# A gated delta rule's heads on one core: modulation rows spread over the chain, the next head's keys ahead of the former head's squares

## What is computed

```python
mod = c_act @ ada_w[layer] + ada_b[layer]        # 6 x 1024 values for each layer
h = rmsnorm(x, g) * (1.0 + scale_m) + shift_m
qkv = silu(conv(h @ w_in)); k = l2norm(k); q = l2norm(q) * 128 ** -0.5
L = where(strict, (k * beta) @ k.T * decay, 0)   # chunks of 64 tokens
u = solve(L + I, v * beta); w = solve(L + I, k * beta * exp(g_cum))
attn = (q @ k.T) * decay
def step(S, ...):                                 # the chain over chunks
    v_new = u_i - w_i @ S
    o_i = q_i @ S + a_i @ v_new
    S = S * gl_i + k_i.T @ v_new
o = rmsnorm(o, norm_g) * silu(gate)               # then o @ w_out
```

## Time and profile before

| what | value |
|---|---|
| median of 3 runs | 2258.55 us (2256.09 to 2258.67) |
| profiled execution, its time | 2256.59 us |
| profiled execution, its span | 2254.8 us |
| PE busy | 2159.7 us, 96% of the span |
| DVE, POOL, ACT busy | 1173.2, 1216.9, 604.2 us |
| mean granted TensorE clock | 0.987 |
| PE's share of the chain that ended last | 86% |

### The profile page before, as it was taken

The page is one execution under the profiler, slowest core; times in us unless marked ns, Lnnn a source line. Parts: engine busy times, 40 slices in busy tenths (PEclk is TensorE's granted clock), DMA queues, the critical chain, the costliest instruction groups (busy, mean ns, idle before and its releaser), DMA issues.

```text
span 2254.8 us, 29386 instructions
## 1 busy us (share of the span) xinstructions
PE 2159.7 (96%) x11960; PEld 1721.9 (76%) x11960; DVE 1173.2 (52%) x1595; ACT 604.2 (27%) x1234; POOL 1216.9 (54%) x687
## 2 busy tenths in 40 slices
PE   8899988889999999998999999999999999999998
PEld 6667666767888887776788888877767778887886
DVE  4666676646827376454532322457755464445332
ACT  3433443323202013343220211332332231002113
POOL 5433232436767777422666666654436266666663
PEclk9999998999999999999999999999999999999999
DMA  8522223225646454210333333322214133333331
GB/s 268 180 64 78 66 89 99 71 62 185 198 159 212 134 196 135 69 49 28 119 99 100 94 99 98 94 85 67 74 45 133 47 97 106 97 94 94 103 103 65
DMA packets 366019, 239.88 MB, mean 106 GB/s; under 512 B 11351, under 2 KB 350653, under 8 KB 365758
## 3 DMA queue, kind: packets, MB, share of 16 engines
q1 hardware_dynamic: 364268, 234.07, 34.6%
q10 hardware_dynamic: 1618, 3.94, 0.5%
HBM read 233.79 MB, written 4.19 MB: 106 GB/s over the span
## 4 chain that ended last, share of the span: by engine, by line
PE 86%; DVE 7%; POOL 2%; ACT 2%; DMA 1%; issue 1%; SPq 1%; ACTq 0%; DVEq 0%; POOLq 0%
PE bank L608 15%; PE bank L610 15%; PE bank L609 15%; PE bank L832 7%; PE bank L627 3%; PE bank L629 3%; PE bank L628 3%; PE mid L898 2%; DVE WIDE L2080 2%; POOL wL L567 1%; PE mid L1406 1%; PE bank L644 1%; PE bank L646 1%; PE bank L645 1%; PE bank L865 1%
## 5 line engine op out<-in xcount | busy, mean ns | idle before, releaser
L565 POOL TENSOR_SCALAR wH<-stage 128x1024 fp32r<-128x1024 f32 (+1 forms) x340 | 388.1, 1141 | 982.8 <-PE bank L610 255.7
L567 POOL TENSOR_TENSOR wL<-stage,wH 128x1024 fp32r<-128x1024 f32 (+1 forms) x340 | 829.7, 2440 | 28.4
L608 PE MATMUL bank<-hH,wH 128*128 128x512 f32 x944 | 368.5, 390 | 0.7 <-DVE A L2157 0.3
L610 PE MATMUL bank<-hH,wL 128*128 128x512 f32 x944 | 367.4, 389 | 0.0
L609 PE MATMUL bank<-hL,wH 128*128 128x512 f32 x944 | 367.3, 389 | 0.0
L608 PE MATMUL bank<-RA,wH 128*128 128x512 f32 (+1 forms) x788 | 284.0, 360 | 6.7 <-DVE RA L2171 3.0
L610 PE MATMUL bank<-RA,wL 128*128 128x512 f32 (+1 forms) x788 | 281.8, 358 | 0.0
L609 PE MATMUL bank<-RA,wH 128*128 128x512 f32 (+1 forms) x788 | 281.8, 358 | 0.0
L608 PEld LDWEIGHTS bank<-hH,wH 128*128 128x128 f32 x944 | 177.2, 188 | 39.8 <-issue 3.2
L609 PEld LDWEIGHTS bank<-hL,wH 128*128 128x128 f32 x944 | 177.2, 188 | 36.9 <-issue 0.2
L610 PEld LDWEIGHTS bank<-hH,wL 128*128 128x128 f32 x944 | 177.2, 188 | 36.8
(11 more groups left out here) (418 smaller groups left out, 3553.2 us busy)
## 6 DMA issues: line engine op xcount, KB each, us to landing
WIDE<-in_ada_t SPq DMA_DIRECT2D x46, 1024.0 KB, 6.1
stage<-in_ffn_w_gate SPq DMA_DIRECT2D x44, 512.0 KB, 3.8
stage<-in_ffn_w_up SPq DMA_DIRECT2D x44, 512.0 KB, 3.9
stage<-in_c_wkv SPq DMA_DIRECT2D x32, 512.0 KB, 3.9
stage<-in_gdn_w_in SPq DMA_DIRECT2D x32, 512.0 KB, 4.2
stage<-in_ffn_w_down SPq DMA_DIRECT2D x32, 512.0 KB, 3.9
stage<-in_o_w_in SPq DMA_DIRECT2D x32, 512.0 KB, 4.0
stage<-in_e_w_in SPq DMA_DIRECT2D x26, 512.0 KB, 3.9
```

The costliest lines, as they stand in the source:

```text
L565: pool.tensor_scalar(high[:, 0:n], raw[:, 0:n], 1.0, 0.0, ALU.mult, ALU.add).then_inc(w_high, 1)
L567: pool.tensor_tensor(low[:, 0:n], raw[:, 0:n], high[:, 0:n].bitcast(F32), ALU.subtract).then_inc(w_split, 1)
L608: pe.matmul(bank[:, 0:n], h[:, k, c], xh[:, k, :], start=first and k == 0, stop=False)
L610: mm = pe.matmul(bank[:, 0:n], l[:, k, c], xh[:, k, :], start=False, stop=last and k == kc - 1)
```

## The change

Five edits:

1. The three modulation rows of a head move on DVE from the head's end into the chain, one behind each state S (`ada_row`).
2. On DVE `key_factors(i + 1)` now comes before `head_sums(i)`; on ACT the former head's square comes after the table load, the logarithm and the two exponentials.
3. On PE the keys' product comes after 8 dense matmuls of the head (12 before) and the former head's squares two dense matmuls behind it, not three ahead of it; 16 dense matmuls stand ahead of the first blocks of the inverse where 24 stood.
4. Each half of a level has 4 dense matmuls for 3 (the last one 3), the end of the head 2 for 3. The sum stays 96.
5. On SP the last modulation group is loaded behind two slabs of `gdn_out`, not ahead of them.

```diff
--- before.py
+++ after.py
@@ -470,8 +470,11 @@
                 head_ada(i)
             for n in range(8, 12):
                 load_kv(n)
-            head_ada(7)
-            residual_loads("gdn_out", a["gdn_w_out"][0], KD)
+            vout = by_cols(a["gdn_w_out"][0])
+            for k in range(KD):
+                load(SLAB0["gdn_out"] + k, vout[k], KD)
+                if k == 1:
+                    head_ada(7)
             kv_spill(0)
             kv_spill(1)
             load_kv(12)
@@ -927,18 +930,18 @@
                         head_units(i + 1, at, at + n)
                     return at + n
 
-                at = dense(9)
+                at = dense(8)
                 if not ahead:
                     kv_slabs("kv0", (0,))
-                if i:
-                    head_squares(i - 1)
-                at = dense(3)
                 pe.wait_ge(g["kb"], i + 1)
                 for t in range(TT):
                     c = slice(t * P, (t + 1) * P)
                     mm = pe.matmul(B3[:, c], k_[:, c], Pm[:, c], start=True, stop=True)
                 mm.then_inc(g["gram"], 1)
-                at = dense(9)
+                at = dense(2)
+                if i:
+                    head_squares(i - 1)
+                at = dense(6)
                 if not ahead:
                     kv_slabs("kv0", (1,))
                 pe.wait_ge(g["silu"], i * 3 + 2)
@@ -961,7 +963,7 @@
                 for n in range(1, 6):
                     pe.wait_ge(g["x"], i * 6 + n)
                     blocks(first_two, LT, own_block, Xs, half_block, 0, 1).then_inc(g["p_ps"], 1)
-                    at = dense(3)
+                    at = dense(4)
                     if not ahead:
                         gdn_out(n - 1, (0,))
                     if n == 1 and i:
@@ -974,7 +976,7 @@
                         pe.wait_ge(g["silu"], i * 3 + 3)
                         pe.wait_ge(g["tok"], 2 * i + 2)
                         turn_over(B7, [vraw[:, t * P:(t + 1) * P] for t in range(TT)]).then_inc(g["vtr"], 1)
-                    at = dense(3)
+                    at = dense(4 if n < 5 else 3)
                     if not ahead:
                         gdn_out(n - 1, (1,))
 
@@ -2328,9 +2330,9 @@
                 own.settle()
                 dve.tensor_tensor(head_out, vn, gs[i % 2], ALU.mult).then_inc(yt_ready, 1)
 
-            def ada_rows(i):
-                for r in range(3 * i, 3 * i + 3):
-                    ada_sum(ADA_HEAD + r // 2, (r % 2,))
+            def ada_row(r):
+
+                ada_sum(ADA_HEAD + r // 2, (r % 2,))
 
             def head(i, ahead):
 
@@ -2411,13 +2413,12 @@
                     ins.then_inc(g["s"], 1)
                     if ahead:
                         conv(i + 1, 2, (2 - t,))
+                    ada_row(3 * i + t)
                 if ahead:
                     decay_rows(i + 1)
                     keys_by_beta(i + 1)
+                    key_factors(i + 1)
                 head_sums(i)
-                if ahead:
-                    key_factors(i + 1)
-                ada_rows(i)
 
             ab = B3[:, 0:128].rearrange("p (t n s h) -> p n s t h", n=2, s=2, h=8)
             dve.wait_ge(g["ab_ps"], 1)
```

## The result

The changed kernel takes 2221.4 us (median; 2217.2 to 2224.4) against 2257.9 for the kernel before: ratio 0.9838, interval [0.9821, 0.9856]. The forecast was 2218, range 2209 to 2233. The profiled execution took 2220.63 us where the forecast's sum gave 2217.1.

A forecast was written before the change was run, and what follows sets the result against it. PE, busy 96% of the span, bounds the kernel; time can be won only where it idles or its clock is low. 35.5 - 3.5 - 0.95 + 7.5 + 1.0 = 39.5 us off 2256.6 gives 2217.1, forecast 2218, range 2209 to 2233.

The forecast's parts named there:

- Part 1: Inverse's first blocks, heads 1 to 6: PE's stall and the low clock behind it go, returning 35.5 us.
- The gap between POOL's instructions: Between POOL's L565 and L567, `head_sums`, third in DVE's queue, gets through; the modulation row, fourth before, had lost.
- Rival (a): `head_sums` loses at POOL's gap; PE waits 1.35 us at the squares in heads 1 to 6; 2227 us, chance 0.30.
- Part 2: Chain, heads 0 to 6: first modulation row meets POOL's L567, new 0.5 us stall at the second state, 3.5 us lost.
- Parts 3, 4 and 6: Levels: 0; head 0: new stall, 0.95 us lost; end of head 7: DVE's L2323 no longer behind rows, 1.0 us gained.
- Part 5: Head 7: PE's 6.01 us wait for `gdn_out`'s second slab goes, 5.5 us, plus 2.0 of low clock: 7.5 us gained.

The follow-up runs named there:

- experiment 6: The changed kernel with the first of the three modulation rows moved ahead of the chain: 2215.3 us, ratio 0.9819 to the kernel before.
- experiment 8: The kernel before, all its orders kept (SP's too), with the modulation rows in the chain and the first row ahead of it: 2214.7 us, ratio 0.9814.
- experiment 1: The kernel before with only the three modulation rows moved into the chain: 2219.9 us, ratio 0.9835.
- experiment 2: The changed kernel with the three modulation rows back at the head's end, so the reordering alone: 2256.2 us, ratio 0.9997.
- experiment 9: The changed kernel with the third modulation row moved from the chain to between `key_factors` and `head_sums` (heads 0 to 6): 2244.0 us, a single profiled execution.
- experiment 10: The kernel before with one modulation row ahead of the chain and the other two left at the head's end: 2218.5 us, ratio 0.9834.
- experiment 4: The changed kernel with ACT's former order, the former head's square ahead of the table load: 2224.8 us, ratio 0.9857.
- experiment 3: The kernel before with only SP's order changed, the last modulation group behind two `gdn_out` slabs: 2258.3 us, ratio 1.0003.
- experiments 7 and 8: The kernel before with rows in the chain, the first ahead of it: with SP's new order 2214.4 us, ratio 0.9813; with SP's old order 2214.7 us, ratio 0.9814.

## Why the prediction was right, point by point

**Part 1, the stall: right.** Rows gone from DVE's way, `L2342` at 4.0 us, sums third at the gap and through, clock back: forecast 35.5 us. By the table heads 1 to 6 went from 48.27 us to 42.33 with the chain's wait taken out (experiment 6): 5.94 each, 35.6 in all. The base of the sum, 42.19 us for a head without a stall, is 42.12 in experiment 8, where PE waits for nothing; so what the kernel before had beyond its stall, which I put down to the low clock, is 1.80 us per head (48.27 - 42.12 - 4.35), not 1.66. The new order costs 0.21 us per head (42.33 against 42.12), where `ors` was put at 0.1: the product of keys by queries starts 0.45 us behind the last of the six dense matmuls (316.05 to 316.50), 0.2 more than a dense one would, and 0.14 us behind the end of ACT's L1709 (316.36). One count in it is wrong without consequence: 15 dense matmuls stood between L845 and the keys' product, not 12; the time taken from the rows, T + 5.92, was right. And one reason in it was superfluous. I counted the earlier keys' product (T + 3.9 for T + 5.9) as a part of the gain; experiment 1 shows that the old order has room for the solve as well, and experiment 2 that the new one alone doesn't show in the kernel's time.

**The gap between POOL's instructions: the outcome right, the rule half right.** Third place wins for the sums (changed kernel) and for a row (experiment 9). Fourth place lost for a row in the kernel before and in experiment 10, and won for the sums in experiment 4, at equal recorded starts. What decides there is not shown. Rival (a) rested on the row's loss, which doesn't carry over to the sums: they got through in fourth place too. Its premise that such a wait leaves the clock alone was wrong for one of 2.1 us in two heads of six (experiment 9); for its own 1.35 us no run shows it.

**Part 2, the chain: right in kind, a little low.** Forecast 0.5 us in 7 heads. The recorded wait is 0.45, but a head is 0.66 us longer by it (42.99 against 42.33 in experiment 6), 4.6 us in all for the 3.5 forecast. It is the meeting with POOL's L570: L2082 takes 3.17 us beside it, and the wait goes when the row does. So the period of 42.99 us, where 42.19 + 0.5 + 0.1 = 42.8 was forecast, is 42.12 + 0.66 + 0.21.

**Parts 3, 4 and 6: right.** No wait in the levels; head 0 waits 0.86 us (0.95 forecast), and is 1.16 us longer by the new order (41.88 against 40.72 in the table). From head 7's first `gdn_out` matmul to its last group before was 448.82 to 486.75, now 416.01 to 451.02: 2.9 us for the 2.0 of clock and 1.0 of rows forecast.

**Part 5, head 7: the wait went, the size was off.** The wait for the slab is gone, and the kv products start 0.64 us later against L845 (0.55 forecast). But that start lies behind a wait of 1.92 us (1.04 before), and the clock fell behind it: the 24 matmuls take 407.95 - 403.49 = 4.46 us where they took 2.95 before; another 0.28 us goes to a bank. So 3.7 us came and not 5.5 ((448.82 - 424.90 before) less (416.01 - 395.80); 424.90 and 395.80 are the starts of L845 and L848). That term was mis-sized by 1.8 us: the sum had priced the later start, but not a low clock behind the longer wait. With the old order, wait and clock stay as before, and the same stretch takes 18.07 us (experiment 8) for 20.21. Of the two reasons given for the earlier load, the rows and the transfer's place in SP's queue, only the first is at work: with the rows at the end the same edit gives 1.3 us in the table and nothing in the kernel's time (experiment 3), and with the rows moved nothing in either (experiments 7 and 8).

**The sum.** The profiled execution is 3.5 us above it: 1.2 in heads 0 to 6, 1.9 in head 7 with `gdn_out` (3.7 + 2.9 us came of 8.5), 0.7 ahead of the heads (the first L845 at 94.56 us, its like at 95.30, in code that the change doesn't touch), less 0.3 behind them. That the last two were so small is luck: the changed kernel's repeat takes 5.7 us more outside the stretch of the table, in the same code.

## What to carry to other kernels

Before moving work to where an engine "has time", look at which other engine's instruction it will meet there: one row of 1.2 us cost 38 us because it pushed the next instructions under a POOL split, and PE waited and ran at a lower clock behind the wait. Undo the parts of a bundle one by one: of five edits one carried all of the gain, the new order took 3 us of it back in the heads, and the kernel with that one edit alone, its first row moved to where DVE idles, is 8 us faster than the bundle beside it (2214.7 against 2222.8). A transfer that lands earlier can cost nearly as much as it gives, when the engine that takes it up blocks another.

## What the runs showed of the hardware that I had not expected

- POOL's two instructions of a split leave a gap of 0.08 us, about which DVE instructions queued behind the first one get through, 0.08 us apart (above L2312 ends its wait there, L2313 and L2319 follow). Three passed every time. At equal recorded starts of a DVE and a POOL instruction either can win: the modulation row lost (3.47 us for 1.28, POOL's 2.39), the sums won (0.69, POOL's 2.92). The Trainium skill (SBUF — State Buffer, Who interferes with whom) has it that such a DVE instruction with two SBUF inputs and a GpSimd one that reads SBUF exclude each other, and that issue order decides which waits; the traces agree (1.24 us became 6.35 under two splits), and show in addition how small a lead is enough, 0.08 us.
- Behind a wait of 1.04 us PE's clock stayed at 2.4 GHz (24 matmuls in 2.95 us, before). Behind one of 1.92 us it was at 1.2 GHz for 3.4 us (matmuls 0.21 us apart from 403.49 to 406.90, then 0.12), and the same 20.2 us for this part of head 7 stand in the repeat and in experiment 6. Behind waits of 2.11 us it was lower in two heads of six (periods of 45.40 and 46.7 us in one execution).
- A wait can cost more than is recorded of it: 0.45 us of idle PE at the second state made a head 0.66 us longer.
